# Mixing panels as one 512-column product: ScalarE empties whole banks, VectorE adds their halves

## The reference

```python
ul = (xl * (1 + sc1_l) + sh1_l) @ w_in        # latent stream, 256 tokens, D_MODEL 2048
uc = (xc * (1 + sc1_c) + sh1_c) @ w_in        # context stream, 256 tokens
ya_c, ya_l = _hgrn_mixer(uc, ul, lb_fwd, lb_bwd, hgrn_norm, need_ctx)   # ends in "* jax.nn.silu(gl)"
yc_c, yc_l = _attention_mixer(uc, ul, attn_sink, need_ctx)              # reads the queries cq
yb_l = _pool_mixer(ul, pool_w, pool_scale)                              # reads the columns B
xl = _layer_norm(ALPHA * xl + g1_l * _merge_branches(ul, (ya_l, yb_l, yc_l), w_branch, w_out), ln1_g, ln1_b)
xl = _layer_norm(ALPHA * xl + g2_l * _sq_relu_mlp(xl * (1 + sc2_l) + sh2_l, w_ff1, w_ff2), ln2_g, ln2_b)
```

## Time and profile before

| | |
|---|---|
| median of 3 runs | 1874.48 us (1874.28 to 1875.72) |
| the profiled execution's own time | 1872.97 us |
| its span | 1871.2 us |
| mean granted TensorE clock | 0.998 of full |
| busy | PE 1844.3 us (99%), DVE 1289.4 (69%), ACT 836.4 (45%), POOL 285.2 (15%) |
| chain that ended last | PE 90%, DVE 4%, DMA 2%, DVE queue 2%, ACT 1% |

### The profile page before, as it was taken

How to read it: one execution, slowest core, us unless ns; L and a number is a source line. 1 busy time by engine, 2 the same in 40 slices (tenths; PEclk the granted TensorE clock), 3 DMA queues, 4 the chain that set the end, 5 groups by cost and what they waited for, 6 DMA issues and landing times.

```text
span 1871.2 us, 24774 instructions
## 1 busy us (share of the span) xinstructions
PE 1844.3 (99%) x10068; PEld 1565.3 (84%) x10068; DVE 1289.4 (69%) x1501; ACT 836.4 (45%) x1030; POOL 285.2 (15%) x163
## 2 busy tenths in 40 slices
PE   7999999999999999999999999999999999999998
PEld 4679888899999788788888888888888888888886
DVE  3357777776869775677767667776686468547887
ACT  3242244465464644544444445443444344434442
POOL 0000000005655360301001000220012001100100
PEclk9999999999999999999999999999999999999999
DMA  9997755543434444475776754565665556656652
GB/s 396 419 353 270 273 202 194 170 175 136 157 104 163 166 168 169 163 269 204 272 268 225 285 208 159 225 247 202 250 242 207 198 207 228 222 194 234 229 185 104
DMA packets 60465, 408.94 MB, mean 219 GB/s; under 512 B 6464, under 2 KB 9280, under 8 KB 12352
## 3 DMA queue, kind: packets, MB, share of 16 engines
q1 hardware_dynamic: 55872, 395.60, 58.3%
q10 hardware_dynamic: 4480, 11.76, 1.7%
HBM read 405.24 MB, written 2.10 MB: 218 GB/s over the span
## 4 chain that ended last, share of the span: by engine, by line
PE 90%; DVE 4%; DMA 2%; DVEq 2%; ACT 1%; issue 0%; SPq 0%; ACTq 0%
PE main L1564 14%; PE main L1565 14%; PE main L1566 14%; PE side L1539 6%; PE main L1539 6%; PE main L1479 5%; PE main L1481 5%; PE main L1480 5%; PE main L1543 3%; PE side L1543 3%; DMA raw<-in_w_ad 2%; DVE wlo L1008 2%; DVEq L1147 1%; PE side L1598 1%; DVE lv L1141 1%; PE main L1620 1%
## 5 line engine op out<-in xcount | busy, mean ns | idle before, releaser
L1008 DVE TENSOR_TENSOR wlo<-raw,whi 128x1024 fp32r<-128x1024 f32 x542 | 703.9, 1326 | 289.3 <-ACT whi L500 288.5
L500 ACT CAST whi<-raw 128x1024 fp32r<-128x1024 f32 x541 | 562.4, 1050 | 699.0 <-PE main L1566 384.9
L1479 PE MATMUL main<-hCL,whi 128*128 128x256 f32 (+1 forms) x768 | 247.7, 323 | 1.0 <-DVE wlo L1008 1.0
L1481 PE MATMUL main<-hCL,wlo 128*128 128x256 f32 (+1 forms) x768 | 244.5, 318 | 0.0
L1480 PE MATMUL main<-hCL,whi 128*128 128x256 f32 (+1 forms) x768 | 244.4, 318 | 0.0
L1029 DVE SCALAR_TENSOR_TENSOR asum<-raw,sm,asum 128x512 f32<-128x512 f32 x240 | 214.5, 894 | 19.9 <-issue 0.9
L1566 PE MATMUL main<-whi,hid 128*128 128x512 f32 x496 | 193.1, 389 | 0.0
L1565 PE MATMUL main<-wlo,hid 128*128 128x512 f32 x496 | 193.0, 389 | 0.0
L1564 PE MATMUL main<-whi,hid 128*128 128x512 f32 x496 | 193.0, 389 | 0.0
L1539 PE MATMUL side<-h,whi 128*128 128x512 f32 x512 | 160.8, 395 | 0.0
L1564 PE MATMUL main<-whi,hCL 128*128 128x512 f32 x384 | 152.3, 397 | 3.5 <-DVE wlo L1008 3.5
(11 more groups left out here) (291 smaller groups left out, 2917.5 us busy)
## 6 DMA issues: line engine op xcount, KB each, us to landing
raw<-in_w_f SPq DMA_DIRECT2D x128, 1024.0 KB, 4.9
raw<-in_w_in SPq DMA_DIRECT2D x103, 1024.0 KB, 4.8
raw<-in_w_ada SPq DMA_DIRECT2D x64, 1024.0 KB, 5.0
raw<-in_w_ad SPq DMA_DIRECT2D x32, 1024.0 KB, 15.4
raw<-in_w_br SPq DMA_DIRECT2D x24, 1024.0 KB, 5.0
raw<-in_w_out SPq DMA_DIRECT2D x16, 1024.0 KB, 4.9
xin<-in_xT SPq DMA_DIRECT2D x8, 512.0 KB, 18.4
raw<-in_w_ck SPq DMA_DIRECT2D x4, 512.0 KB, 14.0
```

What stands on the lines that cost most here:

```text
L500: nc.scalar.copy(half_at(q)[0], slots[slot][:, 2 * h:2 * h + 2]).then_inc(hi_made, 1)
L1008: TT(half_at(q)[1], slots[slot][:, 2 * h:2 * h + 2], half_at(q)[0].bitcast(F32), ALU.subtract).then_inc(lo_made, 1)
L1479: mm(out, w_hi, x_hi, start=start, stop=False)
L1481: return mm(out, w_lo, x_hi, start=False, stop=stop)
```

## The change

In the mixing panels the high weights now multiply both parts of the input in one matmul of 512 columns: a bank holds w_hi·x_hi (+ w_lo·x_hi) in its first 256 columns and w_hi·x_lo in its last 256. ScalarE copies each whole bank to an SBUF tile `zz` (`panel_out`), for all three panels. VectorE adds the two halves of all four banks in one operation (`halves`); for `g` the tanh (ScalarE, from `zz`) and the product (VectorE) follow as one operation each. A semaphore `z_used` keeps `zz` until its readers are done.

```diff
--- before.py
+++ after.py
@@ -233,8 +233,8 @@
     pn.add("query", 0, 4, four, "A")
     pn.add("query", 4, 4, four, "V")
     for i in range(2):
-        for n, who in enumerate("VAV"):
-            pn.add("mix", 12 * i + 4 * n, 4, four, who)
+        for n in range(3):
+            pn.add("mix", 12 * i + 4 * n, 4, four, "A")
     for j in range(3):
         for pp in range(4):
             pn.add("gates", 24 * j + 6 * pp, 4, (0, 1), "A")
@@ -370,6 +370,7 @@
         o_s = [cq[:, 4:8], lv[1][:, 0]]
         o_r = [xb[:, 4:8], lv[1][:, 1]]
 
+        zz = at("zz", [P, 4, 2 * T], 208 * KB)
         avg = at("avg", [P, 4, HD], 208 * KB)
         asum = at("asum", [P, PW], 210 * KB)
         asum_lo = at("asum_lo", [P, PW], 210 * KB, F32R)
...
@@ -647,9 +648,18 @@
                                           side[:, 2 * (k % 2) + tile].rearrange("p (e t) -> p e t", e=4))
                 last.then_inc(lv_cp, 1)
 
+            def panel_out(n):
+                if n:
+                    act.wait_ge(z_used, n)
+                for b in range(4):
+                    blk("mix", 4 * n, b)
+                    last = nc.scalar.copy(zz[:, b], main[:, b])
+                    last.then_inc(freed["A"], 1)
+
             def swap(h):
                 g4 = cq[:, 4 * h:4 * h + 4]
                 drain()
+                act.wait_ge(z_used, 3 * h + 2)
                 nc.scalar.copy(qs[0:64], g4[64:128])
                 nc.scalar.copy(qs[64:128], g4[0:64])
                 nc.scalar.copy(ks[0:64, 0], ak[64:128, h, C:])
@@ -661,20 +671,17 @@
                     split_after("mix", 12 * i + k)
                     if i and k == 0:
                         inverse_rms(0)
-                    if k == 3:
-                        for b in range(4):
-                            blk("mix", 12 * i, b)
-                            A(ya[:, i * 4 + b], main[:, b, 0:T], ACT.Tanh, scale=0.5).then_inc(gs_sig, 1)
-                    if k == 7:
-                        for b in range(4):
-                            blk("mix", 12 * i + 4, b)
-                            nc.scalar.copy(cq[:, i * 4 + b], main[:, b, 0:T]).then_inc(freed["A"], 1)
                     if k in (2, 3):
                         level_scores(i, k - 2)
                     if k < 9:
                         act.wait_ge(lv_arg, i * 9 + k + 1)
                         t = lv[k % 2][:].rearrange("p a e t -> p (a e t)")
                         A(t, t, ACT.Exp).then_inc(lv_exp, 1)
+                    if k == 5:
+                        act.wait_ge(z_sum, i + 1)
+                        A(ya[:, 4 * i:4 * i + 4], zz[:, :, 0:T], ACT.Tanh, scale=0.5).then_inc(gs_sig, 1)
+                    if k in (3, 7):
+                        panel_out(3 * i + k // 4)
                     if k == 9:
                         act.wait_ge(lv_sc, i * 9 + 8)
                         A(lv[1][:, 0], lf[:, 4 * i:4 * i + 4], ACT.Exp)
@@ -682,6 +689,7 @@
                     if k == 11:
                         act.wait_ge(o_ps, i + 1)
                         A(o_s[i], side[:, 2:4].rearrange("p a (c b) -> p (a c) b", b=T), ACT.Square).then_inc(o_sq, 1)
+                        panel_out(3 * i + 2)
             swap(0)
 
             def branch_high(j):
@@ -703,6 +711,8 @@
 
             def gate_out(j, pp):
                 first = 24 * j + 6 * pp
+                if j == pp == 0:
+                    act.wait_ge(z_used, 6)
                 for t in range(2):
                     blk("gates", first, t)
                     A(sg[:, t], main[:, t], ACT.Tanh, scale=0.5).then_inc(freed["A"], 1)
@@ -948,6 +958,7 @@
             rotate(0)
             scores_low(0)
             pool.wait_ge(o_ps, 2)
+            pool.wait_ge(z_used, 6)
             group_values(0)
             def merge(j, pp):
                 for t in range(2):
@@ -1153,6 +1164,10 @@
                     dst = pT[:, tile, :, tile * P:(tile + 1) * P]
                     last = nc.vector.copy_predicated(dst, mk[:, k - 2:k - 1].to_broadcast([P, 4, P]), src)
                 last.then_inc(lv_cp, 1)
+
+            def halves(n, out):
+                dve.wait_ge(freed["A"], PN.own["mix", 4 * n] + 4)
+                return TT(out, zz[:, :, 0:T], zz[:, :, T:2 * T], ALU.add)
 
             def outputs(i):
                 dve.wait_ge(o_rs, i + 1)
@@ -1182,16 +1197,16 @@
                         TT(lv[1][:, 1], lv[1][:, 1], q4, ALU.mult).then_inc(o_op, 1)
                     if 4 <= k < 11:
                         level_scores(i, k - 2)
-                    if k == 3:
-                        for b in range(4):
-                            blk("mix", 12 * i, b)
-                            dve.wait_ge(gs_sig, i * 4 + b + 1)
-                            STT(ya[:, i * 4 + b], ya[:, i * 4 + b], 1.0, main[:, b, 0:T], ALU.add,
-                                ALU.mult).then_inc(freed["V"], 1)
-                    if k == 11:
-                        for b in range(4):
-                            blk("mix", 12 * i + 8, b)
-                            nc.vector.tensor_copy(xb[:, i * 4 + b], main[:, b, 0:T]).then_inc(freed["V"], 1)
+                    if k == 4:
+                        halves(3 * i, zz[:, :, 0:T]).then_inc(z_sum, 1)
+                    if k == 6:
+                        dve.wait_ge(gs_sig, i + 1)
+                        out = ya[:, 4 * i:4 * i + 4]
+                        STT(out, out, 1.0, zz[:, :, 0:T], ALU.add, ALU.mult).then_inc(z_used, 1)
+                    if k == 8:
+                        halves(3 * i + 1, cq[:, 4 * i:4 * i + 4]).then_inc(z_used, 1)
+                    if i and k == 0:
+                        halves(2, xb[:, 0:4]).then_inc(z_used, 1)
 
 
             l1g, l1b = vv[:, V_L1G:V_L1G + KT], vv[:, V_L1B:V_L1B + KT]
@@ -1256,6 +1271,7 @@
                     split_after("gates", 24 * j + k)
                     if j == k == 0:
                         outputs(1)
+                        halves(5, xb[:, 4:8]).then_inc(z_used, 1)
                     if k == 1:
                         branch_low(j)
                     if j and k % 6 in (0, 2):
@@ -1480,6 +1496,9 @@
                 mm(out, w_hi, x_lo, start=False, stop=False)
                 return mm(out, w_lo, x_hi, start=False, stop=stop)
 
+            def parts(ps, b):
+                return ps[:, b].rearrange("p (v t) -> p v t", v=2)
+
             def features(name, first, x, lo, hi, ready=None, between=lambda k: None, middle=lambda k: None):
 
                 for n in range(4):
@@ -1490,11 +1509,21 @@
                         for b in range(4):
                             if n == 0 and h == 0:
                                 bank(name, first, b)
-                            for j in range(2):
-                                kt = 4 * n + 2 * h + j
-                                w_hi, w_lo = (w[:, par, j, P * b:P * (b + 1)] for w in (whi, wlo))
-                                last = three(main[:, b, 0:hi - lo], w_hi, w_lo, x[:, kt, 0, lo:hi], x[:, kt, 1, lo:hi],
-                                             kt == 0, kt == 15)
+                            own = slice(P * b, P * (b + 1))
+                            if name == "mix":
+                                for j in range(2):
+                                    kt = 4 * n + 2 * h + j
+                                    mm(parts(main, b), whi[:, par, j, own], x[:, kt, :, lo:hi],
+                                       start=kt == 0, stop=kt == 15, skip_group_check=True)
+                                for j in range(2):
+                                    kt = 4 * n + 2 * h + j
+                                    last = mm(main[:, b, 0:T], wlo[:, par, j, own], x[:, kt, 0, lo:hi],
+                                              start=False, stop=kt == 15, skip_group_check=True)
+                            else:
+                                for j in range(2):
+                                    kt = 4 * n + 2 * h + j
+                                    last = three(main[:, b, 0:hi - lo], whi[:, par, j, own], wlo[:, par, j, own],
+                                                 x[:, kt, 0, lo:hi], x[:, kt, 1, lo:hi], kt == 0, kt == 15)
                             if n == 3 and h == 1:
                                 last.then_inc(blk_done, 1)
                         if n < 3 or h == 0:
@@ -1502,9 +1531,6 @@
                         if h == 0:
                             middle(n)
                     between(n)
-
-            def parts(ps, b):
-                return ps[:, b].rearrange("p (v t) -> p v t", v=2)
 
             def ahead(name, first, ps, n, h, blocks):
 
```

More of the change, by code:

```diff
@@ L412, in build @@
          at_v, at_sc, at_max, at_exp, at_norm, at_tr, at_cp, at_o, at_y, y_hi, y_lo, pool_diff, pool_ps, pool_y, m_done,
[L413 removed]
+         m_tr, m_hi, m_lo, ax_in, var_in, rs_out, nm_out, h2_tr, h2_hi, h2_lo, x1_done, hid_in, hid_pos, hid_hi, hid_lo, y_out, cleared, sum_hi, sum_lo, centred, diag_made, scaled, row_out, vals_in, qk_hi, qk_lo, z_sum, z_used) = (
```

(2 more changed lines are left out.)

1 line of the change is left out of this document (removed).

## The result

The changed kernel takes 1891.98 us (median of five runs, 1890.55 to 1892.89) against 1874.48: the ratio is 1.009 with an interval of 1.0079 to 1.0102, or +17.5 us. The prediction said slower, with 1881.7 us and a range from 1873 to 1888: the sign was right, the size missed by 10 us, and the time lies 4 us above the range. The profiled execution took 1890.55 us, its span is 1888.4 us; it is the fastest of the five. One execution of e3's kernel ran at a mean granted clock of 0.655 and took 2632.81 us; it is in no comparison.

What follows compares the result with a forecast made beforehand. TensorE, 99% busy, was taken as the bound, so only its own work and its waits count: -4.6 + 10.5 - 1.5 + 2.8 = +7.2 us, giving 1881.7 us, with a range from 1873 to 1888.

Steps and rivals of the forecast that it cites:

- TensorE's own work: Mixing panels: 192 matmul groups at 0.696 us instead of 0.720 save 4.6 us.
- step 3, the query panel's bank: Mixing stage: bank 0's copy stands behind Exp 3, so TensorE waits 2.0 us in each half.
- step 7: Mixing stage: bank 0's copy stands behind Exp 7, so TensorE waits 3.25 us in each half.
- level 8: Mixing stage: VectorE's lateness there goes because TensorE comes 4 us late; -1.5 us for both halves.
- the way into the gate panels: After the mixing stage: rotate(0) contention and an added sum delay gate chunk 2's low parts; +2.8 us, bounds 0 and 5.
- So nothing there: Way into the gate panels: ScalarE's chain ends 9.2 us after the norm sums, when VectorE began L1159 before; no cost.
- What it loses in the mixing stage nothing later gives back: Opening claim about the bound: TensorE time lost in the mixing stage is not recovered later.
- inside these 3.25 us: Step 7: the product from zz pushes level_operands(6) about 0.5 us past chunk 7's end, hidden in the bank wait.
- GpSimd slips under VectorE: Rival, 15%: collisions with VectorE's SBUF operations make GpSimd's arguments late, +5.2 us more, 1886.9 us.
- ScalarE: Trades tanh and copies for about 3 us more per half; 45% busy, so beyond the bank waits it hides.

Runs made afterwards that it cites:

- e3: Changed kernel with swap(0) ahead of the last panel's copies and the last sum of halves behind gate chunk 2's low parts; 1884.27 us.
- e5: Changed kernel with each 512-column product written as two of 256 columns into the bank's two halves; 1892.82 us.
- e7: e4 with each 512-column product written as two of 256 columns; 1881.42 us.
- e1: Changed kernel with ScalarE's four copies of steps 3 and 7 ahead of that step's Exp again; 1885.33 us.
- e2: Changed kernel with the gate's tanh and VectorE's product of g moved from step 6 to step 5; 1894.03 us.
- e9: Changed kernel plus 18 extra 512-column matmuls, result overwritten, where TensorE waits for gate chunk 2; 1887.83 us.
- e4: Changed kernel with the edits of e1, e2 and e3 together; 1879.43 us.
- e6: e4 with VectorE's sums of halves cut to 8 of 256 columns, ScalarE copying the first half instead; 1875.09 us.

## Why the prediction was right in sign and wrong in size

Term by term, from the rows above (us; the right column is 17.2 before rounding):

| Term | forecast | measured |
|---|---|---|
| TensorE's own work | -4.6 | -4.4 (0.4 ahead of level 0, 4.0 behind it) |
| step 3, the query panel's bank | +4.0 | +4.8 |
| step 7; measured: levels 4 to 7 | +6.5 | +8.2, of which 1.6 are the clock |
| level 8; measured: with `outputs` | -1.5 | +0.8 |
| the way into the gate panels | +2.8 | +6.7, of which 2.7 are the clock |
| later | 0 | +0.9 |
| sum | +7.2 | +17.2 |

The steps that failed are two. "So nothing there" on the way into the gate panels took VectorE to be free when ScalarE's chain ended. And in the mixing stage VectorE was given about 0.5 us of lateness inside another wait and nothing ahead of `outputs`; TensorE waited for it 4.5 us ahead of levels and 2.0 ahead of `outputs`. Neither place had a term for the clock.

- **TensorE's own work (-4.6 us)**: the pace was right, 0.696 us a group with a moving operand in two pieces. But it is not a term that can be added to the others: with the product undone, e5 and e7 are slower by 0.8 and 2.0 us and not by 4.6, because the waits shrink as the chunks grow. "What it loses in the mixing stage nothing later gives back" was right; that what it gains can be taken back two steps later was not in the sum.
- **Step 3 (+2.0 each)**: right. 1.79 and 2.56 us; e1 shows that the copies' place makes them.
- **Step 7 (+3.25 each)**: wrong mechanism in the profiled execution, and a size that was near by luck. TensorE did not wait for bank 0 there. It waited 2.06 and 2.05 us ahead of level 6 for VectorE, whose lateness I put at about 0.5 us "inside these 3.25 us". The product from `zz` alone took 2.11 us. e2 shows the bank's limit standing just behind, and in e9 the forecast wait is there, at 1.81 us for 3.25. When e1 took the copies out of the way of both steps, 4.9 us of the stage went, not 10.5, and 1.6 of them were the clock: VectorE's limit stayed.
- **Level 8 (-1.5)**: the wait at level 8 went, as forecast, and came back ahead of `outputs` (0.85 and 1.15 us). Level 7 to `outputs` is 15.8 us before and 15.7 and 16.0 now, although its chunks are shorter.
- **The way into the gate panels (+2.8)**: the largest miss. It cost 6.7. ScalarE's chain was right to 0.1 us. VectorE's two low parts ahead of L1174 fell beside more of `rotate(0)` (5.88 us for 4.56; L1174 started 1.4 us late), the four products took 2.6 us more where I had 1 to 2 for them and the low part together, the sum 1.2: together 5.2. And 2.7 us are the lower clock behind the wait, which no part of the prediction allowed for.
- **The rivals**: "GpSimd slips under VectorE" had the right pair of engines and, in the changed kernel, the wrong victim. GpSimd's arguments 7 took no longer; VectorE's operations did. Only in the reordered kernels was GpSimd late (`q_lo`, 8.91 us). The Trainium skill (SBUF — State Buffer, SBUF: two separate sides) has the two share a port pair. The rows agree in this: L1174 with a PSUM input keeps 1.21 us beside GpSimd, and L1177 with SBUF inputs alone goes from 0.42 to 1.07 us each.
- **ScalarE**: no wait was traced to its added work, only to its order, as forecast.

Taken together: order made 12.6 us of the 17.5 (changed kernel to e4), of which about 4.3 are the lower clock behind waits that order made, and the sums on VectorE made 4.3 more (e4 to e6), a part of it through GpSimd. The saving on TensorE, which was to pay for it, is hidden where VectorE binds. How much of VectorE's load is its own work and how much the collision with GpSimd is open: no run took one without the other. No run here was faster than the kernel before by more than can be measured.

## What to carry to other kernels

An engine that is busy 69% of the span can be full in the very stage where its partner's work is cut (here 41.2 of 42.0 us). Ask of that stage, not of the page, what the saving will run into, and compare the length of a stretch between two fixed points in both kernels. Price an operation on VectorE by what GpSimd does beside it at its new place, and ask of every wait that goes which one stands right behind it. When a move takes a collision away from one engine, look for it on the other. And keep TensorE fed: behind some of the waits of 1.8 to 4.7 us here the lower clock cost another 1.6 to 2.7 us.

## What was not expected of the hardware

- **The clock behind a wait.** In a kernel that is 98% busy on TensorE, single waits of 1.8 to 4.7 us were followed by about 3 to 6 us at a granted clock of 0.50, which is 1.2 GHz (mean 0.57 of full in 488 to 492; 13 matmuls at 0.427 us for 0.227). Not every such wait was: of two waits of 2.05 and 2.06 us at the same place of the two halves one was, one was not; why is open. Filling the wait of 4.73 us with useless matmuls took the fall behind it away and won 2.5 us there; the median fell by 4.1.
- **Useless work can be free.** The 18 matmuls of e9 took 4.24 us and delayed nothing measurable: the next chunk started 18.6 us after the norm sums with them, and without them at the same 18.6.
- **VectorE beside GpSimd.** The 256-column products of L1177 took 1.07 us each beside `rotate(0)` and 0.42 without it, while an operation of 1024 columns with one PSUM input (L1174) took 1.21 and 1.22 us. In the other direction, a low part of 1024 columns on GpSimd took 3.25 us in the kernel before and 8.91 in e4.
